# A conditional section moved from one attention stage to an earlier one, on GpSimd

## The reference, cut to what matters

```
mod = silu(c) @ w_ada[l] + b_ada[l]
shift1, scale1, gate1, shift2, scale2, gate2 = split(mod, 6)
h = rms_norm(x, norm1_g) * (1 + scale1) + shift1
... MLA attention and differential attention, both on h @ w_in ...
x = x + gate1 * mix
h2 = rms_norm(x, norm2_g) * (1 + scale2) + shift2
x = x + gate2 * hier_moe(h2)
```

## Time and profile before

| what | us |
|---|---|
| median of 3 runs | 2610.27 |
| the profiled execution | 2606.18 |
| its span in the profile | 2604.5 |
| TensorE busy in the span | 2372.6 |
| VectorE busy | 1730.4 |
| ScalarE busy | 1227.9 |
| GpSimd busy | 450.2 |

### The profile page before, as it was taken

The page is one execution under the profiler, slowest core; times in us unless marked ns, Lnnn a source line. Parts: engine busy times, 40 slices in busy tenths (PEclk is TensorE's granted clock), DMA queues, the critical chain, the costliest instruction groups (busy, mean ns, idle before and its releaser), DMA issues. The chain is left out here.

```text
span 2604.5 us, 31503 instructions
## 1 busy us (share of the span) xinstructions
PE 2372.6 (91%) x10766; PEld 1905.8 (73%) x10766; DVE 1730.4 (66%) x1998; ACT 1227.9 (47%) x1643; POOL 450.2 (17%) x396
## 2 busy tenths in 40 slices
PE   4989987888698599999999769999999999999998
PEld 4767765777477487777877658887878888888886
DVE  6378885666485799999999675445357666653344
ACT  5246664656321477676767461111553333332322
POOL 0000000887500010000000110000013332311100
PEclk7989998999797699999999879999999999999999
DMA  6131120339465699999999854443423232245453
GB/s 246 32 118 47 44 88 30 106 98 338 145 199 178 251 399 398 399 398 399 399 398 399 323 193 129 121 122 103 123 65 89 74 95 72 85 155 160 150 171 112
DMA packets 266072, 485.30 MB, mean 186 GB/s; under 512 B 19633, under 2 KB 125566, under 8 KB 265470
## 3 DMA queue, kind: packets, MB, share of 16 engines
q1 hardware_dynamic: 232734, 364.37, 40.2%
q0 software_dynamic: 26912, 98.62, 11.2%
q10 hardware_dynamic: 6336, 21.11, 2.0%
HBM read 402.25 MB, written 76.55 MB: 184 GB/s over the span
## 5 line engine op out<-in xcount | busy, mean ns | idle before, releaser
L2151 DVE TENSOR_TENSOR e_w<-e_raw,e_w 128x1024 fp32r<-128x1024 f32 x384 | 442.5, 1219 | 46.2 <-ACT e_w L2215 45.6
L2215 ACT ACTIVATE e_w<-e_raw 128x1024 fp32r<-128x1024 f32 x384 | 376.7, 1051 | 176.0 <-PE e_pgu L111 142.9
L111 PE MATMUL e_pgu<-e_w,e_xt 128*128 128x512 f32 x1536 | 369.6, 397 | 10.6 <-DVE e_w L2151 5.3
L111 PEld LDWEIGHTS e_pgu<-e_w,e_xt 128*128 128x128 f32 x1536 | 286.4, 189 | 85.3 <-DVE e_w L2151 17.8
L111 PE MATMUL s_ps<-h,s_w 128*128 128x512 f32 x1152 | 268.4, 394 | 2.1 <-DVE h L2579 2.1
L111 PEld LDWEIGHTS s_ps<-h,s_w 128*128 128x128 f32 x1152 | 218.0, 190 | 48.6 <-DVE h L2579 2.3
L111 PE MATMUL w_ps<-w_out,w_ring 128*128 128x512 f32 x1056 | 245.4, 392 | 1.9 <-DVE w_ring L3231 1.9
L111 PE MATMUL w_ps<-y 128*128 128x512 f32 x1056 | 240.1, 389 | 1.4 <-DVE w_o_full L3396 1.0
L111 PEld LDWEIGHTS w_ps<-w_out,w_ring 128*128 128x128 f32 x1056 | 199.3, 189 | 45.0 <-DVE w_out L3238 2.3
L111 PEld LDWEIGHTS w_ps<-y 128*128 128x128 f32 x1056 | 198.0, 188 | 43.5 <-issue 1.4
L111 PE MATMUL w_ps<-y,w_ring 128*128 128x512 f32 x816 | 195.9, 398 | 3.3 <-ACT w_h L3027 3.0
(11 more groups left out here) (430 smaller groups left out, 3916.0 us busy)
## 6 DMA issues: line engine op xcount, KB each, us to landing
e_raw<-in_w_expert_gate_dram SPq DMA_DIRECT2D x128, 512.0 KB, 10.9
e_raw<-in_w_expert_up_dram SPq DMA_DIRECT2D x128, 512.0 KB, 8.1
e_raw<-in_w_expert_down_dram SPq DMA_DIRECT2D x128, 512.0 KB, 10.5
w_raw<-in_ffn_w_gate_up_dram SPq DMA_DIRECT2D x48, 512.0 KB, 6.1
w_o_full<-in_ffn_w_down_dram SPq DMA_DIRECT2D x44, 512.0 KB, 4.0
y_rows<-am_zrow SPq DMA_DIRECT2D x4, 4352.0 KB, 35.9
raw_rows<-in_w_ada_dram POOLq DMA_DIRECT2D x32, 512.0 KB, 4.1
y_rows<-e_yo ACTq DMA_DIRECT2D x32, 512.0 KB, 6.3
```

The source lines that it names most:

```text
L111: o = pe.matmul(out, stat[i], mov[j], start=start and n == 0, stop=stop and n == 2)
L2151: dve.tensor_tensor(w[1][:, slot % CUT], raw[:, slot], w[0][:, slot % CUT].bitcast(F32), ALU.subtract).then_inc(low, 1)
L2215: act.activation(w[0][:, slot % CUT], raw[:, slot], ACT.Copy).then_inc(high, 1)
```

## The change

The fourth late section (index 3, `gate2`) leaves `mla_attention`, which gets the first three jobs only. It is computed by GpSimd in `diff_attention`, ahead of the two latent loads, in four groups of 256 columns: a group has 9 pieces of 128 x 256, so there are 36 pieces. The buffers are new and small (`narrow_rows` of 2 x 256 and `narrow` of 256 elements for each partition). The order within a piece is that of `mla_attention`. The program begins when the low part of h is done (`h_low` at 8), and it waits for its last store before the latent loads.

```diff
-def diff_attention(nc, g, a, h_t, h_at):
+def diff_attention(nc, g, a, h_t, h_at, jobs):
...
+        narrow_rows = sb("narrow_rows", [P, 2, QUARTER])
+        narrow = sb("narrow", [P, QUARTER])
+        pieces = PIECE * len(jobs) * (D // QUARTER)
...
             @block.gpsimd
             def _(pool):
+                def job_of(t):
+                    u = t // PIECE
+                    w, b, cond, section, at = jobs[u // (D // QUARTER)]
+                    c0 = (u % (D // QUARTER)) * QUARTER
+                    return w, b, cond, section * D + c0, at, slice(c0, c0 + QUARTER)
+
+                def load(t):
+                    w, b, _, c0, _, _ = job_of(t)
+                    k, cols = t % PIECE, slice(c0, c0 + QUARTER)
+                    if k < KD:
+                        pool.dma_start(narrow_rows[:, t % 2, :], w[0].rearrange("(p k) n -> p k n", k=KD)[:, k, cols]).then_inc(part_in[t % 2], 16)
+                    else:
+                        pool.dma_start(narrow_rows[0:1, t % 2, :], b[0:1, cols]).then_inc(part_in[t % 2], 16)
+
+                pool.wait_ge(h_low, KD)
+                load(0)
+                load(1)
+                for t in range(pieces):
+                    u, k, row = t // PIECE, t % PIECE, narrow_rows[:, t % 2, :]
+                    _, _, cond, _, at, cols = job_of(t)
+                    pool.wait_ge(part_in[t % 2], 16 * (t // 2 + 1))
+                    if t:
+                        pool.wait_ge(step, t)
+                    if k == 0:
+                        if u:
+                            pool.wait_ge(acc_out, 16 * u)
+                        pool.tensor_scalar(narrow[:], row, cond[:, 0:1], None, ALU.mult).then_inc(step, 1)
+                    elif k < KD:
+                        pool.tensor_scalar(row, row, cond[:, k:k + 1], None, ALU.mult).then_inc(part_scaled, 1)
+                        pool.wait_ge(part_scaled, (KD - 1) * u + k)
+                        pool.tensor_tensor(narrow[:], narrow[:], row, ALU.add).then_inc(step, 1)
+                    else:
+                        pool.tensor_tensor(narrow[0:1, :], narrow[0:1, :], row[0:1, :], ALU.add).then_inc(step, 1)
+                    pool.wait_ge(step, t + 1)
+                    if t + 2 < pieces:
+                        load(t + 2)
+                    if k == KD:
+                        pool.dma_start(g.acc_dram[at][:, cols], narrow[:]).then_inc(acc_out, 16)
+                pool.wait_ge(acc_out, 16 * (pieces // PIECE))
                 pool.wait_ge(lat_out, 32)
                 pool.wait_ge(scored1, NT * (HEADS - 1))
...
-                diff_attention(nc, g, a, h_t, h_at)
+                diff_attention(nc, g, a, h_t, h_at, first_sections[3:])
...
-            mla_attention(nc, g, a, finished, first_sections)
+            mla_attention(nc, g, a, finished, first_sections[0:3])
```

More of the change, by code:

```diff
@@ L97 @@
 PIECE = KD + 1
+QUARTER = D // 4
 def swap_halves(sp, to, src, rows, done):
@@ L142, in diff_attention @@
                  "maxed nmax expd summed weighted combined probs turned pt_high pt_low vturned v_high v_low pv taken o_out "
-                 "lproj kproj lat_raw squared ssq rooted recip normed lat_high lat_low lat_out kpe_angle kpe_sum kpe_high kpe_low")
+                 "lproj kproj lat_raw squared ssq rooted recip normed lat_high lat_low lat_out kpe_angle kpe_sum kpe_high kpe_low "
+                 "part_in0 part_in1 part_scaled step acc_out")
         (w_in0, w_in1, w_high, w_low, w_used, proj, pj_out, swapped, cos_done, sin_done, roped, qk_high, qk_ready, scored0, scored1,
@@ L146, in diff_attention @@
          o_out, lproj, kproj, lat_raw, squared, ssq, rooted, recip, normed, lat_high, lat_low, lat_out, kpe_angle, kpe_sum, kpe_high,
-         kpe_low) = sems(nc, g, " ".join("ad_" + s for s in names.split()))
-        w_in = (w_in0, w_in1)
+         kpe_low, part_in0, part_in1, part_scaled, step, acc_out) = sems(nc, g, " ".join("ad_" + s for s in names.split()))
+        w_in, part_in = (w_in0, w_in1), (part_in0, part_in1)
         names = ("ident_in c_in lam_in rows_in rows_clear cs_in lat_w_in x_in0 x_in1 x_in2 x_in3 x_in4 x_in5 x_in6 x_in7 "
```

## The result

The changed kernel takes 2593.07 us (median of 4 runs, 2590.93 to 2594.44), beside 2608.93 us for the kernel before, measured with it (4 runs, 2607.0 to 2611.44): ratio 0.9939 (95% interval [0.9924, 0.9955]), 15.9 us or 0.6% less. Forecast were 2603.4 us and a gain of 6.9. The profiled execution took 2594.44 us with a span of 2592.8, which is 11.7 us less than that of before.

A forecast was written before the change was run, and what follows sets the result against it. GpSimd's fourth section alone was taken to set MLA's end. Span 2604.5 less 13.9 there plus 7 of VectorE's loss gave 2597.6; the median 2610.27 less 6.9 gave 2603.4 us, range 2596 to 2610.

The forecast's parts named there:

- The first term: End of MLA: without the fourth section and with earlier `w_out` loads, the next block starts 13.9 us sooner (11.7 to 15.6).
- The pause of 0.4 us: End of MLA: VectorE idles only 0.43 us, as at the end of attention_out, instead of 11.72 us.
- the hidden `dmix` loads: End of MLA: four 512 KB loads issued until 660.17 us land in 5.7 us each with 17 us left.
- GpSimd's time: Differential attention: 0.88 us a multiplication, 0.76 an addition, 2.66 a piece, 25.7 a group; work ends at about 175 us.
- VectorE's loss: Differential attention: GpSimd's pieces hold VectorE off, 5.8 us between 112.4 and 160.8 us, 1 behind; taken as 7.
- The alternation: Second block at 1930 us: VectorE and GpSimd take turns, a GpSimd addition 3.39 instead of 1.30, VectorE's next 3.27 instead of 2.29.
- the way from the profile to the median: Whole kernel: the profiled execution lies 4.1 us under the runs' median, so 2599.3 us becomes 2603.4.
- B: Differential attention: GpSimd gets in only where VectorE pauses, loss 1.6 us, 2598.0 us in all; chance 0.25.
- mine: Whole kernel: 13.9 us gained at MLA's end, 7 lost by VectorE, 2603.4 us; chance 0.47.
- C: Differential attention: multiplications hold VectorE off for their full length, 11.2 us lost, 2607.6 us in all; chance 0.18.
- D: Differential attention: each GpSimd instruction pushes VectorE back by its full length, 36 us lost, 2632 us; chance 0.07.
- E: End of MLA: the end does not move because something else (`dmix`) is late, 2617 us; chance 0.03.

The follow-up runs named there:

- after: The changed kernel's first measurement and profile, against the kernel before: 2593.07 us, ratio 0.9939.
- after again: The changed kernel unaltered, measured a second time against the kernel before: 2595.31 us, ratio 0.9956.
- after once more: The changed kernel unaltered, a third measurement against the kernel before, in the same rounds as split: 2590.5 us, ratio 0.9948.
- additions only: The changed kernel without the 28 multiplications of pieces 1 to 7 in the differential attention; one run: 2591.58 us.
- late loads: The changed kernel with the `w_out` loads held until VectorE's last MLA instruction; one run: 2597.84 us.
- left out: The changed kernel with the fourth section computed nowhere, one DMA copy filling its place: 2593.49 us, ratio 0.9949 to before.
- two moved: The changed kernel with the third section moved to the differential attention too, 72 narrow pieces, two sections left to MLA: 2596.89 us, ratio 0.9961.
- multiplications only: The changed kernel without the 32 narrow additions in the differential attention; one run: 2589.98 us.
- eighths: The changed kernel with eight groups of 128 columns instead of four of 256, 72 pieces; one run: 2592.77 us.
- split: The changed kernel with columns 0 to 511 in the differential attention, the other half as one 512-column job ending MLA: 2591.53 us, ratio 0.994 to before.
- held: The changed kernel with GpSimd's narrow section begun only after five steps of first scores: 2594.76 us, ratio 0.9953.

## Why the prediction was wrong

The direction and the mechanism were right; a cost was set too high, and the rest of the miss lies in which executions the medians caught.

**The first term held**: 13.9 us forecast, 13.95 or 13.96 measured in ten of the table's eleven executions, and 9.96 in the one where I took the early loads away. The pause of 0.4 us and the hidden `dmix` loads came as the rows had said.

**GpSimd's time held in its parts, not in its end**: 0.94 and 0.73 us against 0.88 and 0.76. The work ended at 183 instead of 175 us because the narrow instructions wait for VectorE (multiplications between 112 and 161 us take 1309 ns in the mean) and one store took over 6.85 us to land. Nobody waits for either.

**The step that failed is VectorE's loss, 7 us forecast**: the term was 5.8 us between 112 and 161 us and 1 behind. Measured were 3.05, 3.21 and 3.21 in three profiles of the changed program. Behind 161 VectorE's instructions are 0.1, 0.6 and 0.1 us longer, and no time is lost: from 159.56 to 300.34 the shift even falls, by 0.3 to 0.9 us. The alternation that I took from the earlier trace rows is real. Shared out over the forecast's 15 pieces, the 5.8 us are 0.27 for an addition and 0.12 for a multiplication. The additions' price held (0.24). The multiplications' did not (0.05): their 0.33 us of hold was scaled down from one 1024-column row. And 12 multiplications and 11 additions lie in the stretch instead of 15 and 15, because GpSimd itself waits there. That accounts for 3.2 against 5.8. With 3.1 for 5.8 and nothing for the last 1, the sum is 2604.5 - 13.9 + 3.1 = 2593.7 us, and the span was 2592.8.

**The second step that failed is the way from the profile to the median.** The forecast for the profiled execution was 2599.3 us, and 2594.44 came, 4.9 us less; the loss explains 3.9 of these. The other 5.5 of the 10.3 us come from carrying the distance between profile and median over: I added 4.1 us for it, while the median of the changed kernel's runs lies 1.4 under its profiled execution. With the loss at 3.1 and this step left as it was, the forecast would have been 2599.5 us. That distance belongs to single executions, not to a kernel; the kernel before itself came to 2605.86 and 2605.68 us in nine runs each, 4.5 us under the median of three from which I started. I had allowed 1.7 us for such things.

**Where executions of one program part.** Three profiles of the changed program have spans of 2592.8, 2593.5 and 2588.2 us. Their shifts differ by under 1 us at 159.56 and by 6.4 at 676.69. Some of it comes between 300 and 452 us, and its cause stays open. The rest is MLA, where wide pieces of GpSimd run beside VectorE in every version. Two things change from execution to execution there. The first is the granted clock of MLA's first steps. Here are the same matmuls (112 or 113 in the records) in the kernel before, after, after again and after once more:

```profile
452.00:480.00 28.00, 23.22 (x112) 17.30 (x110) 14.32 (x22) 16.16 (x23) 23.13 (x14) 0.95 0.48 139
...
458.40:488.50 30.10, 27.16 (x113) 19.99 (x111) 14.37 (x22) 16.31 (x23) 25.14 (x15) 0.80 0.48 144
...
455.10:483.30 28.20, 23.22 (x113) 17.34 (x111) 14.36 (x22) 16.19 (x23) 23.32 (x14) 0.96 0.47 138
...
453.90:484.00 30.10, 27.18 (x113) 19.93 (x111) 14.39 (x22) 16.33 (x23) 25.16 (x15) 0.81 0.48 143
```

At 0.80 or 0.81 the stretch takes 2.1 us longer than before, at 0.96 it takes 0.2. GpSimd has started with the block either way, so the second thing is what its pieces meet from then on. One of the instructions that change, in the kernel before and in after:

```profile
504.74 3.27 DVE L1296 TENSOR_TENSOR mf_w<-w_mla,mf_w 128x896 fp32r<-128x896 f32 x1
...
511.75 1.09 DVE L1340 TENSOR_TENSOR mf_w<-w_mla,mf_w 128x896 fp32r<-128x896 f32 x1
```

Against before, VectorE's instructions from 452 to 677 us are 4.7 us shorter in sum in after, 4.4 shorter in after once more, but 0.9 longer in after again. From about 480 us to 676.69 the shift falls by 3.6 and 5.5 in the first two and by 0.2 in the third. The two other versions that show 0.80 there, additions only and late loads, behave like the first two (shift down by 3.6 and 3.5), left out, at 0.91, nearly so (3.4), and two moved, multiplications only, eighths and split (0.96) like the third (within 0.3). Held (0.95) does not fit: 3.5 us shorter, with no low clock in those steps. So a slower start there was more than paid back by cheaper meetings. That is read from traces, and no version was made to test it.

The mean of the three measured gains is 13.9 us (15.9, 10.6, 15.2), where the traces give 13.95 - 3.1 = 10.8. The one profile of before is an execution of the costly kind. Whether its runs are mostly so and the changed kernel's less often, or the 3 us are chance, stays open. Left out, with no loss between 112 and 161 us, came to 0.9949 as well. And not all of it lies in MLA: held falls another 4.0 us and multiplications only 3.2 behind 692.78, in stretches that no version changes.

**The rivals**: B, at 1.6 us, and mine, at 7, enclose the 3.1 measured; nearer to B in size, while its mechanism, GpSimd getting in only where VectorE pauses, is refuted by L803's wait of 0.53 us. C, D and E are refuted: 0.77 us in sum for 16 multiplications, a shift of 3 us and not 36, and a block that starts 0.39 us behind VectorE's last instruction.

## What to carry to other kernels

Small elementwise work of GpSimd may lie beside a busy VectorE if its pieces are short: what VectorE paid here was part of one piece's addition at each meeting, and in the one profile with pieces of half the width it paid less in sum, although there were twice as many. Read who comes last at the end of a block, engine by engine: what that one still has to do, and what is queued behind it, is the gain, and it is exhausted once another engine is last. For an effect of a few microseconds compare matched instructions of two traces and take the same kernel's profile more than once; the distance of one profile from its median is no constant to be carried over. Where two engines that don't wait for each other share a stretch, look at which of their instructions met in that execution before you put a difference down to the change.

## What was not expected of the hardware

A GpSimd multiplication by a column of scalars (one full input) and an addition of two tiles behave unlike each other beside VectorE: both wait for it (0.94 to 2.00 us, 0.73 to 1.14), but a narrow one of the first kind costs VectorE 0.05 us in the mean and one of the second 0.24. GpSimd's plain lengths have a fixed part that grows in weight with narrowness: the multiplication took 2.85 us for 1024 columns and 0.94 for 256; the addition 2.40 and 0.73, and for 128 columns 0.46 (eighths, where it did not wait). VectorE's tiny 128x1 instructions with two SBUF inputs pay as well: that of L830, 220 ns in the mean between 200 and 300 us in the changed kernel, takes 328 in two moved, where GpSimd works beside it.
